# A decoder step on one core: the gathered rows of the down weights spread over 29 quads instead of 26, and the routing's small tables in a PSUM bank

## The reference, cut to what matters

```python
q = (xb @ peer_wq).reshape(PEER_BLOCK, PEER_HEADS, 2, PEER_HALF)
s = jnp.einsum('thcd,hckd->thck', q, subkeys)
sv, si = lax.top_k(s, PEER_TOPK)                       # 16 of 128 keys, for each half
cand = sv[:, :, 0, :, None] + sv[:, :, 1, None, :]     # 256 candidates
cidx = si[:, :, 0, :, None] * PEER_N_KEYS + si[:, :, 1, None, :]
top_s, sel = lax.top_k(cand, PEER_TOPK)                # 16 experts of 16384, per token and head
expert = jnp.take_along_axis(cidx, sel, axis=-1)
g = jax.nn.softmax(top_s, axis=-1)
act = jax.nn.gelu(jnp.einsum('thkd,td->thk', peer_u[expert], xb))
out = jnp.einsum('thk,thkd->td', g * act, peer_v[expert])
```

## Time and profile before

| | |
|---|---|
| median of three runs | 4547.12 us (4541.0 to 4558.92) |
| the profiled execution, its own time | 4554.33 us |
| its span | 4552.6 us, granted clock 0.988 |
| TensorE busy | 4382.5 us, 96% |
| VectorE, ScalarE, GpSimd busy | 2475.2, 1527.4, 2816.6 us |
| HBM | 935 MB read, 95 MB written, 226 GB/s over the span |

### The profile page before, as it was taken

How to read it: one execution, slowest core, us unless ns; L and a number is a source line. 1 busy time by engine, 2 the same in 40 slices (tenths; PEclk the granted TensorE clock), 3 DMA queues, 4 the chain that set the end, 5 groups by cost and what they waited for, 6 DMA issues and landing times.

```text
span 4552.6 us, 75504 instructions
## 1 busy us (share of the span) xinstructions
PE 4382.5 (96%) x28787; PEld 4142.6 (91%) x28787; DVE 2475.2 (54%) x3222; ACT 1527.4 (34%) x1921; POOL 2816.6 (62%) x1440
## 2 busy tenths in 40 slices
PE   7999999999999989999999998999999999999998
PEld 7899999899888978888888898999999999999998
DVE  5632333413102165555555865777777677776656
ACT  4422222223222244444443553333333333333332
POOL 6933222243222457777777787788888788886643
PEclk9999999999999999999999999999999999999999
DMA  6643333434564256556656559999999899999854
GB/s 212 213 105 99 112 111 105 155 105 144 195 204 169 90 176 183 182 182 182 183 182 186 171 189 347 361 361 355 356 354 357 302 355 360 357 358 339 324 189 158
DMA packets 493934, 1032.09 MB, mean 227 GB/s; under 512 B 55776, under 2 KB 285280, under 8 KB 461024
## 3 DMA queue, kind: packets, MB, share of 16 engines
q1 hardware_dynamic: 316528, 592.77, 39.8%
q0 software_dynamic: 45056, 268.60, 15.2%
q10 hardware_dynamic: 132208, 168.75, 10.6%
HBM read 935.26 MB, written 94.73 MB: 226 GB/s over the span
## 4 chain that ended last, share of the span: by engine, by line
issue 35%; POOL 28%; PE 25%; DMA 7%; DVE 2%; ACT 2%; POOLq 0%; ACTq 0%; SPq 0%; DVEq 0%
POOL WS L478 26%; PE PS L592 13%; PE PS L1039 12%; DMA RAW<-in_vE 6%; POOL AR L501 2%; ACT WS L1074 1%; POOL ROWS L511 1%; DMA pmap<-ROWS 0%; DVE AR L2057 0%; DMA ROWS<-in_vE,AR 0%; DVE AR L2041 0%; PE PS L995 0%; DVE AR L2245 0%; DVE AR L2052 0%; POOLq L477 0%
## 5 line engine op out<-in xcount | busy, mean ns | idle before, releaser
L592 PE MATMUL PS<-HL,WS 128*128 128x288 f32 (+2 forms) x16896 | 2392.6, 303 | 63.6 <-POOL WS L478 31.6
L592 PEld LDWEIGHTS PS<-HL,WS 128*128 128x128 f32 x16896 | 2349.1, 190 | 84.4 <-issue 33.9
L478 POOL TENSOR_TENSOR WS<-RAW,WS 128x1024 fp32r<-128x1024 f32 x600 | 1473.9, 2467 | 1409.9 <-ACT WS L1074 1406.6
L1074 ACT ACTIVATE WS<-RAW 128x1024 fp32r<-128x1024 f32 x600 | 615.1, 1055 | 1204.0 <-PE PS L592 445.5
L1039 PE MATMUL PS<-WW,WS 128*128 128x320 f32 x6144 | 930.5, 313 | 59.7 <-POOL WS L478 50.2
L1039 PEld LDWEIGHTS PS<-WW,WS 128*128 128x128 f32 x6144 | 911.6, 190 | 77.4 <-issue 46.5
L942 PE MATMUL PS<-WS,HL 128*128 128x512 f32 x3072 | 702.0, 390 | 3.0 <-POOL WS L478 3.0
L942 PEld LDWEIGHTS PS<-WS,HL 128*128 128x128 f32 x3072 | 576.3, 188 | 122.2 <-POOL WS L478 3.4
L478 POOL TENSOR_TENSOR WS<-CS,WS 128x1024 fp32r<-128x1024 f32 x200 | 492.1, 2460 | 136.0 <-ACT WS L1074 134.2
L2114 DVE SCALAR_TENSOR_TENSOR PS<-ROWS,AR,PS 128x2048 f32<-128x2048 f32 x206 | 483.5, 2347 | 12.9 <-DMA ROWS<-in_vE,AR 12.5
L2129 DVE TENSOR_TENSOR AR<-AR,PS 128x320 f32<-128x320 f32 x512 | 247.5, 484 | 317.6 <-PE PS L1039 316.3
(11 more groups left out here) (209 smaller groups left out, 2503.0 us busy)
## 6 DMA issues: line engine op xcount, KB each, us to landing
RAW<-in_uT SPq DMA_DIRECT2D x256, 512.0 KB, 4.5
RAW<-in_w_lin SPq DMA_DIRECT2D x216, 512.0 KB, 3.5
CS<-in_uT SPq DMA_DIRECT2D x128, 512.0 KB, 4.7
AR<-in_uT SPq DMA_DIRECT2D x128, 512.0 KB, 5.0
RAW<-in_vE SPq DMA_DIRECT2D x128, 512.0 KB, 7.9
CS<-in_vE SPq DMA_DIRECT2D x64, 512.0 KB, 5.1
AR<-in_vE SPq DMA_DIRECT2D x64, 512.0 KB, 9.4
AR<-in_w_lin SPq DMA_DIRECT2D x48, 512.0 KB, 4.3
```

The costliest lines, as they stand in the source:

```text
L478: pool.tensor_tensor(WS[:, k, 1, :], raw(k, many, late), WS[:, k, 0, :].bitcast(F32), ALU.subtract)\
L592: ins = mm(to, WS[:, slot + hf, wp, k * P:(k + 1) * P], x, start=first and (wp, xp) == (0, 0), stop=last and wp == 1, skip_group_check=True)
L1074: copy = lambda out, in_, **kw: act.activation(out, in_, ACT.Identity, **kw)
```

## The change

- **Rows.** A table gives each quad its number of rows. Tile 0 takes quads 0 to 13 (8, then nine each, in quads 9 to 12 ten each, 8 in quad 13), tile 1 takes quads 14 to 28 (nine each, in quad 26 ten, in the down-only quads 27 and 28 five each). Row j keeps its place k = 8j//5 in a full quad; where a quad has nine rows, the one after k = 14 is gone. In the down-only quads a row is issued after each of the blocks 0, 1, 2, 4, 5. VectorE adds them after d = 2, 5, 8, 11, 14.
- **Turning back and final norm.** Tile 0 turns back in quad 13, tile 1 in quad 29 after d = 4. Its X add comes after d = 6 of quad 29, its squares in the second half of quad 29, their sums after d = 2 to 6 of quad 30, the sum over partitions after d = 8 of quad 30, the factor after d = 12 and 15 of quad 30, the spread in quad 31, and the scaling in quad 31 after d = 3 to 10 instead of 0 to 7.
- **Routing.** SIF, TAF and a copy of half of SV lie in PSUM bank 7. The scores are packed in 1280 consecutive floats of banks 4 to 6, so that bank 7 is free. One copy of 128x80 is added per head.

```diff
-KR = 2 * NB
-QR = -(-P // KR)
+QR0, QR1 = 14, 15
+ROWS_IN = [8] + [9] * 8 + [10] * 4 + [8] + [9] * 12 + [10, 5, 5]
-V_USED = (0, V_MAP // KR, QR, QR + 6, QR + 10)
+V_USED = (0, 11, QR0, QR0 + 7, QR0 + 11)
+T0 = QR0 + QR1
+def rows_of(i):
+    if i >= T0:
+        return 0, 0, 0
+    c = int(i >= QR0)
+    return c, sum(ROWS_IN[QR0 * c:i]), ROWS_IN[i]
...
-        SI, SIF = ar(2720, 2, TILES, TOPK).bitcast(U32), ar(2880, 2, TILES, TOPK)
+        SI = ar(2720, 2, TILES, TOPK).bitcast(U32)
+        SIF = bank(7, 2 * TILES * TOPK, off=0).rearrange("p (c t k) -> p c t k", c=2, t=TILES)
+        TAF = bank(7, 2 * TILES * TOPK, off=2 * TILES * TOPK).rearrange("p (c n) -> p c n", c=2)
+        SVB = bank(7, TILES * TOPK, off=4 * TILES * TOPK).rearrange("p (t k) -> p t k", t=TILES)
...
             for i in range(QT):
-                c, first = i // QR, i % QR * KR
+                c, first, count = rows_of(i)
                 for k in range(16):
                     ...
-                    for j in range(KR):
-                        if c < 2 and first + j < P and k == (8 * j // 5 if i else j + 6):
+                    for j in range(count):
+                        if k == (8 * j // 5 if i else j + 6):
...
-            with pool.Fori(0, NQ - QT) as i:
-                for k in (0, 1, 2, 4, 5, 6):
-                    low_part(i * 8 + (H_V + k // 4 * 4), k % 4, late=True)
+            for i in range(QT, NQ):
+                c, first, count = rows_of(i)
+                for j, k in enumerate((0, 1, 2, 4, 5, 6)):
+                    low_part(H_V + 8 * (i - QT) + k // 4 * 4, k % 4, late=True)
+                    if j < count:
+                        row(c, first + j)
...
             for i in range(QT, NQ):
                 down(12 * QT + 6 * (i - QT), 4 * QT + 2 * (i - QT), 0, i, (WW, WW2)[(i - QT + 1) % 2],
-                     between={QT + 2: tiles_sum, QT + 3: tiles_factors}.get(i))
+                     between={T0: (4, lambda: rows_back(2)), T0 + 1: (8, tiles_sum), T0 + 2: (2, tiles_factors)}.get(i))
...
             for i in range(QT - 1, NQ):
                 n = H_V + 8 * (i - QT)
+                if i == T0:
+                    rows_back(2)
...
-            with step.loop(EH, 16) as h:
+            with step.loop(EH, 17) as h:
                 ...
                 dve.tensor_copy(SIF, SI)
+                link(dve.tensor_copy(SVB, SV[:, 1]))
                 for t in range(TILES):
                     ins = tt(CAND[:, t, :]..., wide(SV[:, 0, t, :], TOPK),
-                             SV[:, 1, t, :].unsqueeze(1).to_broadcast([P, TOPK, TOPK]), ALU.add)
+                             SVB[:, t, :].unsqueeze(1).to_broadcast([P, TOPK, TOPK]), ALU.add)
...
             def tiles_scaled(d):
-                if d == 0:
+                if d == 3:
                     dve.wait_ge(S["rb_done"], 4)
-                for b in (2 * d, 2 * d + 1):
-                    if b < KB:
+                for b in (2 * d - 6, 2 * d - 5):
+                    if 0 <= b < KB:
...
                     next_w(i + 1, d)
-                    if i == QT + 1:
+                    if d % 3 == 2:
+                        add_rows(i, (d // 3,))
+                    if i == T0 and d == 6:
+                        add_tile(1).then_inc(S["tiles_added"], 1)
+                    if i == T0 + 1:
                         tiles_squares(d)
-                    if i == QT + 2:
                         tiles_factor(d)
```

More of the change, by code:

```diff
@@ L1025, in tiles_factors, with rows_back @@
                 mm(bank(7, NG), ONES[:, 0, :], TRD, start=True, stop=True).then_inc(S["rb_done"], 1)
+            def rows_back(tiles_done):
+                pe.wait_ge(S["rows_evac"], tiles_done)
+                for c in range(KB):
+                    at = 2048 + P * c
+                    turned = pe.transpose(PS[:, at:at + P], AE[:, P * c:P * (c + 1)], IDENT)
+                turned.then_inc(S["back_done"], 1)
             def down(i12, i4, first, i, W, back=False, between=None):
@@ L1043, in down @@
                             ins.then_inc(S["v_done"], 1)
-                        if between and d == 2:
-                            between()
+                        if between and d == between[0]:
+                            between[1]()
                         if back and d == 13:
-                            pe.wait_ge(S["rows_evac"], back)
-                            for c in range(KB):
-                                at = 2048 + P * c
-                                turned = pe.transpose(PS[:, at:at + P], AE[:, P * c:P * (c + 1)], IDENT)
-                            turned.then_inc(S["back_done"], 1)
+                            rows_back(back)
                     ins.then_inc(S["used"], 2)
@@ L1057, in quad @@
                 down(i * 12, i * 4, 8, i, WW, back)
-            for c in range(2):
-                with pe.Fori(0, QR - 1) as i:
-                    quad(i + c * QR)
-                quad(c * QR + QR - 1, back=c + 1)
-            for i in range(2 * QR, QT):
+            with pe.Fori(0, QR0 - 1) as i:
                 quad(i)
+            quad(QR0 - 1, back=1)
+            with pe.Fori(0, QT - QR0) as i:
+                quad(i + QR0)
             for i in range(QT, NQ):
                 down(12 * QT + 6 * (i - QT), 4 * QT + 2 * (i - QT), 0, i, (WW, WW2)[(i - QT + 1) % 2],
-                     between={QT + 2: tiles_sum, QT + 3: tiles_factors}.get(i))
+                     between={T0: (4, lambda: rows_back(2)), T0 + 1: (8, tiles_sum), T0 + 2: (2, tiles_factors)}.get(i))
             token_sums(4, ND)
@@ L1522, in gelu_tokens @@
                         act.wait_ge(S["cand_done"], h + 1)
[L1523 removed]
+                        copy(SC.rearrange("p c t n -> p (c t n)"), ACC[:, 0:2 * RT5])\
                             .then_inc(S["sc_evac"], 1)
@@ L1644, in next_highs, with rows_back @@
                 high2(n + (2 * q + 4), 2 * (q % 2), late=True)
+            def rows_back(c):
+                act.wait_ge(S["row_done"], P * c + 1)
+                copy(AE, ACC).then_inc(S["rows_evac"], 1)
             def quad(i, back=False, first=False):
@@ L1654, in quad @@
                     if back and q == 2:
-                        act.wait_ge(S["row_done"], P * back + 1)
-                        copy(AE, ACC).then_inc(S["rows_evac"], 1)
+                        rows_back(back)
             load_x3(0, 3, "in_x0")
@@ L1661, in _ @@
             quad(0, first=True)
-            for c in range(2):
-                with act.Fori(0, QR - 2 + c) as i:
-                    quad(i + (1 - c + c * QR))
-                quad(c * QR + QR - 1, back=c + 1)
-            for i in range(2 * QR, QT - 1):
-                quad(i)
+            with act.Fori(0, QR0 - 2) as i:
+                quad(i + 1)
+            quad(QR0 - 1, back=1)
+            with act.Fori(0, QT - 1 - QR0) as i:
+                quad(i + QR0)
             ups(QT - 1)
@@ L2116, in add_rows @@
             def add_rows(i, js):
-                c, first = i // QR, i % QR * KR
+                c, first, count = rows_of(i)
                 for j in js:
-                    if c < 2 and first + j < P:
+                    if j < count:
                         add_row(c, first + j)
```

41 lines of the change are left out of this document (19 added, 22 removed).

## The result

The changed kernel takes 4586.57 us (median of four runs, 4584.21 to 4589.62). The kernel before took 4551.98 us beside it (4541.0 to 4558.92). The ratio is 1.0074, with a 95% interval of 1.0057 to 1.009. The forecast was 4549 us in a range of 4526 to 4568, with 0.08 for slower by over half a percent: the time lies 19 us outside the range. The sum was +1.6 us, the rest of six terms that nearly cancelled, against 34.6 measured; that the sign agrees is chance. The profiled execution took 4589.62 us, 35.3 us more than that of before.

A forecast was written before the change was run, and what follows sets the result against it. TensorE is busy 96% of the span; the landing of two loads was taken to set the quads. Terms -4 - 1.4 + 5 + 5 + 2 - 5 = +1.6 us on 4547.12 gave 4549 us, range 4526 to 4568.

The forecast's parts named there:

- Rows in quads 1 to 25: Most of these quads lose the row after k = 14, issued too late to delay their two loads: -4 us.
- The second wait in quads 15 to 21: Sign: TensorE's wait ahead of a quad's third quarter should still be near 1.1 us on average.
- pool of bytes: Bandwidth as one pool: one MB less per quad is 5%, 0.6 us a quad, 12 us in 20 quads.
- faster rival: With 5% fewer bytes the two loads land in time and the second waits go: 4508 us; chance 0.12 with what lies near.
- landings under 11 us: Sign that decides for the rival of 4508 us: the two loads land in under 11 us in most quads.
- Quad 26: It gets ten rows and is priced like quads 22 to 25, plus 0.3 us for VectorE's products: +5 us.
- Quads 27 and 28: Five rows each in the down-only quads; waits for VectorE and GpSimd of 2.5 us a quad: +5 us.
- slower rival: Each of the eight quarters of quads 27 and 28 begins 2.5 us late: 32 us instead of 5, 4576 us; chance 0.08.
- The final norm: Quads 29 to 31: square-root wait moves at 0, squares' sums meeting products +0.5, quad 31's scaling +1.5; together +2 us.
- Routing: Last head: TensorE's wait of 2.95 us and its clock cost go, the first map product still waits 0.5 us: -5 us.
- Quad 0: Eight rows instead of ten shorten its last two waits, 0.93 and 0.48 us behind VectorE: -1.4 us.
- Turning back: Moves from quad 25 to quad 29 with all its instructions: 0 us.

The follow-up runs named there:

- e10: The changed kernel plus a blank VectorE add, no row gathered, where its nine-row quads have no tenth add; 4572.6 us, ratio 1.0033.
- e2: The kernel before, with the loads of the next quad's map and gelu values issued after the second gelu store instead of the third; 4522.21 us, ratio 0.9941.
- e13: The changed kernel with the fifth slot of its nine-row quads empty instead of the tenth, and a blank VectorE add in that slot; 4548.83 us, ratio 0.9973.
- e1: The kernel before with the routing part of the change alone; 4548.49 us, ratio 0.9987.
- e9: The kernel before with the routing part of the change and the maps' loads issued earlier; 4516.76 us, ratio 0.9917.

## Why the prediction was wrong

**Rows in quads 1 to 25, -4 us (bounds 0 and -12): measured +11.9. This step failed.** The argument was that the tenth gather "can't delay the two loads of its own quad", that by the next quad "the backlog has drained", and so "the term is 0". It was right about the transfer: where only the tenth gather is gone (e10, with VectorE's work kept), quads 1 to 21 take 1241.3 us against 1237.7, no gain beyond what such profiles spread. The cost came in by a part of the row that the step left out, its add on VectorE. VectorE's total was counted as free; its place was not looked at. The end of the tenth add lies past the quad's start and keeps the subtraction out of GpSimd's way; the blank add gives 14 us back in both settings (11 and 19 by the ratios). The second wait in quads 15 to 21, forecast "near 1.1 us", was 1.6 us on average, and 0.8 before. The bounds had no case of a loss, although the row of before that shows the products at 4.50 us for four, beside a subtraction of 1.22, was there to be read.

**Why the pool of bytes gave nothing.** The faster rival (bytes set the landing, 4508) was right in its mechanism: e2 and e13 show that a megabyte less beside the two loads takes their waits away. It was wrong about the change, which takes its megabyte away elsewhere: its sign, landings under 11 us, is absent (11.7 and 12.0 us on average in the nine-row quads).

**Quad 26, +5 us (bounds +1 and +8): measured +14.3. This step failed too.** It was priced like quads 22 to 25, with 0.3 us for the products of quad 27. But here the products for quad 27 stand among the sums, and so a map load that lands 19.8 us after its issue stops VectorE and TensorE for 9.26 us, plus 3.5 us at the low clock behind it (156 matmuls in 26.39 us; at the 82.94 us for 564 of the earlier trace rows they take 22.9). The step counted the weight loads that rows delay and left out the load on ScalarE's queue, though the trace of before had its time beside rows, 18.0 us on average.

**Quads 27 and 28, +5 us: measured +6.7.** The stepping held: VectorE's waits come to 1.93 us in quad 27 and 1.95 in quad 28 (1.8 was forecast), and GpSimd's to 0.55 and 0.46. The slower rival (each quarter late by 2.5 us) did not occur: the loads issued as the two quads begin took 11.1 and 11.5 us, and no quarter began 2.5 us late.

**The final norm, +2 us: measured +5.0.** The mechanism was named (sums of squares meeting the products), and mis-sized: 0.5 was taken where 4.27 us of wait and its clock cost came. Missing in the sum was GpSimd's pair of low parts, beside which two instructions of VectorE took 2.2 us longer each. In quad 31 the wait is 1.18 us (0.40 before), where 1.5 was taken.

**Routing, -5 us: measured -6.9** at the place, and 7 in e1's profile; by two pairs of medians -4.4 (e1) and -5.5 (e9 against e2). The step held and was a little short: the first map product, given 0.5 us, needed none, though the second waited for 1.22. VectorE's ten products save 15.4 us a head, where "over 12" was read from rows that give 11.8 at least. **Quad 0, -1.4 us: measured +3.3.** The step looked at its last two waits alone. With the change and with the routing alone, quad 0 takes back 3.3 and 5.3 us of what is gained ahead of it. The other changed kernels have the same code in quad 0 and take 75.7 to 78.6 us for it, the change 77.7 and before 74.3; what paces it was not tried. **Turning back, 0: measured 0.**

**The range.** It was said to be the bounds of the terms, "not all at once". Added up, they are all at once: about -22 and +21 us on 4547. The measured time is outside because four terms went past their bounds, the rows by 12 us, quad 26 by 6, quad 0 and the norm by 3 each.

## What to carry over

An instruction on an engine with half its time free is still part of the schedule: before taking work away, look at what will move up into its place and what that meets. When transfers are thinned, take them away beside the load that is waited for; the total and the average share said nothing of it here. And where a stage gets new transfers, list every load that lands in it, on each queue, with the instruction behind which the sums stand.

## What the runs showed of the hardware

- A VectorE tensor_tensor with both inputs in SBUF beside a GpSimd low part: 1.22 us becomes 3.93, 0.48 becomes 2.73. The routing's product of 128x256: 412 ns on average with one input in PSUM against 2526 with both in SBUF (80 of them in each kernel).
- The other way round, an indirect issue on GpSimd took 0.95 to 0.97 us where no such instruction of VectorE overlapped it (208 in quads 1 to 21 of the change), and up to 1.76 us where one did; every issue over 1 us (98) overlapped one.
- Adding 2.35 us of work to VectorE in each of 20 quads made two kernels 14 us faster each by the medians, 11 and 19 by the ratios.
- A 640 KB load on ScalarE's queue landed 19.8 us after its issue with the engines at 0.94 to 0.97 of their time, and 6.3 us after it in the same quad when they moved 192 GB/s.
